# Moving the first outputs' turns to the end of a step in the second kind of heads

## The reference

```python
o_a = diff_attention(q_a, ka_all, va_all, lam)
o_a = rmsnorm(o_a, lw['subln_a']) * (1.0 - l_init)
o_c = softmax_attention(q_c, kc_all, vc_all)
o_b = b_b * conv
y = jnp.concatenate([o_a, o_b, o_c], axis=-1) @ lw['w_out']
```

## Time and profile before

| what | value |
|---|---|
| median of three runs | 2001.78 us |
| the profiled execution, its own time | 2002.92 us |
| its span, first to last instruction | 2000.9 us |
| mean granted TensorE clock | 0.970 |
| PE busy | 1843.9 us, 92% of the span |
| DVE busy | 1407.7 us, 70% |
| ACT busy | 1029.8 us, 51% |
| POOL busy | 333.8 us, 17% |

### The profile page before, as it was taken

How to read it: one execution, slowest core, us unless ns; L and a number is a source line. 1 busy time by engine, 2 the same in 40 slices (tenths; PEclk the granted TensorE clock), 3 DMA queues, 4 the chain that set the end, 5 groups by cost and what they waited for, 6 DMA issues and landing times.

```text
span 2000.9 us, 28755 instructions
## 1 busy us (share of the span) xinstructions
PE 1843.9 (92%) x11276; PEld 1655.3 (83%) x11276; DVE 1407.7 (70%) x2014; ACT 1029.8 (51%) x1401; POOL 333.8 (17%) x507
## 2 busy tenths in 40 slices
PE   5999789799999999998997888897999999999994
PEld 3996777698999999998996776795788888888883
DVE  5487885547666566546477875446988888888887
ACT  4245686524211211124236776434777777777772
POOL 0083540111000000001084531100000000000002
PEclk8999799999999999999998899997999999999997
DMA  9225200023454444421230000007999999999995
GB/s 333 69 94 216 85 1 1 33 74 126 160 168 136 159 138 158 142 80 48 71 100 27 1 1 1 2 22 299 388 405 394 414 403 397 395 392 405 377 387 218
DMA packets 112439, 366.21 MB, mean 183 GB/s; under 512 B 7457, under 2 KB 65217, under 8 KB 85937
## 3 DMA queue, kind: packets, MB, share of 16 engines
q1 hardware_dynamic: 94448, 303.50, 40.5%
q0 software_dynamic: 13536, 48.39, 6.9%
q10 hardware_dynamic: 4320, 12.49, 1.6%
HBM read 349.23 MB, written 15.12 MB: 182 GB/s over the span
## 4 chain that ended last, share of the span: by engine, by line
PE 78%; DVE 9%; ACT 6%; DMA 3%; issue 2%; POOL 1%; SPq 0%; DVEq 0%; POOLq 0%; ACTq 0%
PE PS L2449 28%; PE PS L2338 26%; PE PS L2006 8%; PE PS L2393 5%; PE PS L2430 4%; PE PS L2094 3%; ACT E L909 3%; PE PS L2118 2%; DVE NM L1356 2%; PE PS L2129 2%; ACT PT L914 1%; DVE KCn L1303 1%; DMA araw<-in_w_ada_head 1%; DVE SS L1286 1%; DMA raw<-in_w_ada_head 1%
## 5 line engine op out<-in xcount | busy, mean ns | idle before, releaser
L2449 PEld LDWEIGHTS PS<-H,split 128*128 128x128 f32 x2304 | 339.0, 188 | 2.8 <-issue 1.7
L2449 PE MATMUL PS<-H,split 128*128 128x320 f32 x2304 | 340.7, 310 | 0.5 <-DVE H L1903 0.5
L1088 ACT CAST split<-raw 128x2048 fp32r<-128x2048 f32 (+2 forms) x64 | 112.8, 1763 | 225.9 <-PE PS L2449 174.3
L1550 DVE TENSOR_TENSOR msplit<-raw,msplit 128x2048 fp32r<-128x2048 f32 x82 | 187.9, 2292 | 36.7 <-ACT msplit L1045 36.6
L1639 DVE TENSOR_TENSOR split<-raw,split 128x2048 fp32r<-128x2048 f32 (+2 forms) x64 | 136.5, 2133 | 107.4 <-ACT split L1088 106.9
L1550 DVE TENSOR_TENSOR split<-raw,split 128x2048 fp32r<-128x2048 f32 x82 | 186.8, 2289 | 18.8 <-ACT split L1045 18.8
L2338 PE MATMUL PS<-split,HT 128*128 128x512 f32 x816 | 195.8, 396 | 2.8 <-DVE HT L1529 2.4
L1045 ACT CAST msplit<-raw 128x2048 fp32r<-128x2048 f32 x82 | 157.0, 1915 | 69.9 <-PE PS L2338 61.2
L2338 PE MATMUL PS<-msplit,HT 128*128 128x512 f32 x816 | 191.1, 390 | 1.6 <-DVE msplit L1550 1.6
L2338 PEld LDWEIGHTS PS<-msplit,HT 128*128 128x128 f32 x816 | 152.9, 188 | 34.1 <-DVE msplit L1550 2.4
L2338 PEld LDWEIGHTS PS<-split,HT 128*128 128x128 f32 x816 | 151.9, 189 | 34.1 <-DVE HT L1529 2.8
(11 more groups left out here) (350 smaller groups left out, 3090.9 us busy)
## 6 DMA issues: line engine op xcount, KB each, us to landing
raw<-in_moe_w_gate SPq DMA_DIRECT2D x55, 1024.0 KB, 7.6
raw<-in_moe_w_down SPq DMA_DIRECT2D x55, 1024.0 KB, 8.2
raw<-in_moe_w_up SPq DMA_DIRECT2D x54, 1024.0 KB, 7.5
DOTW<-in_w_ada_rows POOLq DMA_DIRECT2D x56, 512.0 KB, 4.0
raw<-in_w_ada_head SPq DMA_DIRECT2D x16, 1024.0 KB, 6.8
mraw<-in_moe_w_up SPq DMA_DIRECT2D x14, 1024.0 KB, 7.8
mraw<-in_moe_w_gate SPq DMA_DIRECT2D x13, 1024.0 KB, 7.4
mraw<-in_moe_w_down SPq DMA_DIRECT2D x13, 1024.0 KB, 8.4
```

The source lines that it names most:

```text
L1088: A.copy(split[u % 2][:, 0, 0:w], src[:, 0:w]).then_inc(S["split_hi"], 1)
L1550: V.tensor_tensor(msplit[n % M_SPLIT][:, 1, :], mraw[n % M_RAW], msplit[n % M_SPLIT][:, 0, :].bitcast(f32), ALU.subtract).then_inc(S["piec ...
L2449: ins = T.matmul(PS[:, 4 * (u % 2) + 2 * c + hf, 0:HALF], W[:, w, k, c * P:(c + 1) * P], A(a, k, hf), start=(k == 0 and w == 0 and a == 0) ...
```

## The change

In the second kind of heads

- on PE `mix_turn` of tile t stands at the end of step 53 + t, behind the E-turn, and no longer at its start, ahead of the scores;
- on ACT `mix_hi` of tile t stands in step 54 + t behind the copy of `PT`, and no longer at the start of step 53 + t;
- on DVE `mix_lo` of tile t stands at the end of step 54 + t, and no longer at the end of step 53 + t;
- on ACT the cast of the convolution stands at the end of step 52, ahead of all casts of tiles, and no longer at the start of step 58, behind them.

The waits themselves and the work are the same.

```diff
@@ ACT
             for k in range(-2, ITEMS):
                 hg = groups_at(k, 0)
-                if 0 <= k - K_MIX < NT:
-                    mix_hi(k - K_MIX, 1, MIX_A, k - K_MIX)
-                if k == K_MIX + NT:
-                    A.copy(MIX[:, mix_slots(l, 0, MIX_CONV), :], CONV[:, :, :]).then_inc(S["conv_hi"], 1)
                 if k + 2 < ITEMS:
...
                     A.copy(PT[k % 2][:, 0:cols], PSF[:, 3072:3072 + cols]).then_inc(S["pt_out"], 1)
+                if 0 <= k - K_MIX - 1 < NT:
+                    mix_hi(k - K_MIX - 1, 1, MIX_A, k - K_MIX - 1)
                 if (hg := groups_at(k, 1)) is not None:
                     turn_out(*hg)
+                if k == K_MIX - 1:
+                    A.copy(MIX[:, mix_slots(l, 0, MIX_CONV), :], CONV[:, :, :]).then_inc(S["conv_hi"], 1)
@@ DVE
-                if 0 <= k - K_MIX < NT:
-                    mix_lo(k - K_MIX, 1, MIX_A, k - K_MIX)
+                if 0 <= k - K_MIX - 1 < NT:
+                    mix_lo(k - K_MIX - 1, 1, MIX_A, k - K_MIX - 1)
@@ PE
             for k in range(-2, ITEMS + 1):
-                if 0 <= k - K_MIX < NT:
-                    t = k - K_MIX
-                    if t == 0:
-                        pe.wait_ge(S["turn_out"], (l + 1) * TURNS)
-                    else:
-                        pe.wait_ge(S["mix_lo"], l * 10 + t)
-                    pe.wait_ge(S["subln_gained"], l * NT + t + 1)
-                    mix_turn(t, 1, QA[:, t, :])
                 if k + 2 < ITEMS:
...
                     turn_group(*hg)
+                if 0 <= k - K_MIX < NT:
+                    t = k - K_MIX
+                    if t == 0:
+                        pe.wait_ge(S["turn_out"], (l + 1) * TURNS)
+                    else:
+                        pe.wait_ge(S["mix_lo"], l * 10 + t)
+                    pe.wait_ge(S["subln_gained"], l * NT + t + 1)
+                    mix_turn(t, 1, QA[:, t, :])
```

## The result

The changed kernel takes 2023.42 us in the median of four runs (2022.70 to 2026.08), against 2003.04 for the kernel before, which was run once more beside it. The ratio is 1.0105 (95% interval 1.0091 to 1.0119), so it is slower by some 21 us, where 14.5 were forecast. The direction and the two causes, a longer loop of waits and a clock that falls, were right; the clock's share was too small. The forecast time of 2016.3 is 7 us short, and the measured time lies at the upper end of the range, 2023.5 (1.0105 times 2003.04 is 2024.1).

The account below looks back on a forecast made before the run. A loop of waits in attention steps 52 to 59, not a busy engine, was taken as the bound. Loop 3.25 and clock 4.0 us, twice, make 14.5 us on the median of 2001.78: 2016.3 us, range 2007.5 to 2023.5.

Parts of the forecast that it names:

- the loop: Steps 52 to 59: scores, maximum, exponential, copy, cast, remainder, turn, scores; 5.01 us a step, costing 3.25 us a layer.
- The links: Seven waits from scores round to the next scores: 1.28, 0.86, 0.79, 0.59, 0.50, 0.60 and 0.39 us.
- The convolution's cast: ACT, end of step 52: the moved cast is hidden behind the maximum, by 0.1 us only.
- The clock: PE's idle stretches let its clock fall in both layers, between 380 and 387: 4.0 us a layer, bounds 1.95 and 7.5.
- my bound of 7.5: Upper bound a layer if the low clock lasts into the projection: last turns 0.5, `OC` turns 1.2, dense products about 2.
- That the clock holds: Rival for steps 52 to 59: clock stays full, so only the loop's 6.5 us are lost: 2008.3 us; chance 0.18.
- The faster case: Rival: ACT casts the tile ahead of the exponential, so step 53's gain mostly stays: 1.6 us a layer, 1998.6 us; chance 0.05.
- Near-cancellation: Rival: loop binds in steps 55 and 56 only, step 57's wait is hidden: 0 to 3 us, 2003 us; chance 0.07.
- That the convolution's cast does the harm: Rival: the cast at the end of step 52 isn't hidden and delays step 53, adding up to 1.3 us a layer.
- The forecast's own case: Loop and clock together in both layers: 14.5 us slower, bounds 2010.7 to 2023.3 us; chance 0.70.

Follow-up runs that it names:

- filler_full: Changed kernel plus dummy identity turns (8, 16, 20, 10) on PE ahead of the four waits for a tile's remainder: 2009.76 us, ratio 1.0030.
- conv_first_only: Kernel before with only the convolution's cast moved to the end of step 52: 2002.07 us, ratio 0.9997.
- cast_first_remainder_last: Changed kernel with only ACT's tile cast put to the step's start, ahead of the exponential: 1999.28 us, ratio 0.9982; measured again, 2001.16 us, 0.9998.
- conv_back: Changed kernel with the convolution's cast put back to the start of step 58: 2022.04 us, ratio 1.0087.
- cast_first: Changed kernel with ACT's tile cast at the step's start and DVE's remainder right behind the maximum: 2000.99 us, ratio 0.9989.
- before_remainder_early: Kernel before with only DVE's tile remainder moved right behind the maximum of its step: 2002.80 us, ratio 1.0002.
- cast_first_split_late: cast_first with DVE's remainder of the projection's first weights moved from the end of step 55 to that of step 57: 2003.52 us, ratio 1.0004.

## Why the prediction was right or wrong

**The bound and the loop: right.** The links summed to 5.01 us, and filler_full has 5.01. The first steps went as worked through: scores of item 56 3.91 us behind the pair product of step 52 (365.00 to 368.91; 370.83 less 366.87 is 3.96), scores of item 57 8.79 behind it (8.76 worked out), turn of tile 2 13.43 behind it (13.38). PE's waits in layer 0 were 1.33, 2.56, 2.40 and 1.76 us, forecast as 1.3, 2.5, 3.2 and 1.7. The third was shorter only because the scores and turns ahead of it took longer at the lower clock; in layer 1, at full clock, it was 3.30, and its turn came 18.90 us into the stretch (18.78 worked out). The loop's price was forecast at 3.25 us a layer, and it is 3.4.

**The convolution's cast: right**, covered by 0.07 us (0.1 worked out).

**The clock: right that it falls, and mis-sized by a third** (8.0 us forecast, 11.7 measured). This is the step that failed: "So the bounds are 1.95 and 7.5 a layer; I take 4.0". Taking filler_full as the kernel at full clock, layer 0 has 28.26 - 25.34 = 2.9 us in the stretch. From the last pair product to the turns of `OC` it has another 1.5 (4.61 us against 3.13), and from there to the long run of the projection's products another 1.9 (5.27, as 397.87 to 403.14, against 3.37): 6.3 us. Layer 1, in the same way, has 1.6 + 1.5 + 2.3 = 5.4.

What was wrong is that I priced one fall, 6.8 us long as in rows 6, and let it end there. The first fall came about where it was placed: on the time scale of rows 4 it began at 379.9 in layer 0 and at 386.3 in layer 1, where I had said between 380 and 387. It lasted 10.3 us in one and 3.4 in the other. Full clock did come back, at 388.3 in layer 0 and 1289.4 in layer 1. But with the wait ahead of the turn of tile 4 (1.76 us), PE was busy only 1.65 of the next 3.4 us, 1.56 in layer 1, and the clock fell again at 391.7 and 1292.8, for 10.2 us in both layers. This second fall reached through the turns of `OC` into the projection, whose dense work nothing hides. It costs 0.3 + 1.5 + 1.9 = 3.7 us in layer 0 and 1.5 + 2.3 = 3.8 in layer 1; the first costs the remaining 2.6 and 1.6. So 4.0 was too much for the one fall that it priced (3.8 by my terms), and had nothing for the second; the two errors partly cancel, and the number is better than its reason. One price was low as well: the pair product takes 1.1 us more at the lower clock (2.40 for 1.31), where I had 0.95. The parts for the case that the low clock reaches the projection stood in my bound of 7.5, and I left them out.

How a fall comes out isn't fixed by the schedule alone: both layers ran the same work with the same waits up to the turn of tile 2 (13.43 and 13.42 us into the stretch), and the clock fell 13.0 us into the stretch in layer 0 and 19.4 in layer 1. The first fall cost 2.6 us in one and 1.6 in the other, and nothing that I read told which.

The Trainium skill's page "TensorE: Matmul & The Clock Gate" (Part 1: The HAM clock gate) calls the throttled state the default and activity what releases it. The measured term, 11.7 us for both layers, is on the side of that rule; without it the sum would have stopped at the loop's 6.8.

**The sum.** Loop 6.8 and clock 11.7 are 18.5 us. This is what the trace has lost from the pair product of step 52 to the projection, 9.7 us in layer 0 and 8.8 in layer 1, and no second check of it: the clock's part is what the loop leaves over. The span grew by 20.5. The remaining 2 us lie outside, where I expected no change, and I can't tell them from scatter: the two executions already differ by 1.87 us where they reach the stretch, the other way, ahead of anything that was changed, and by some 4 us behind it. What the entry to the experts took (end of the last product of `MIX` to the first of `MAT`) was 91.7 us before, 93.5 after, and 89.7 in conv_first_only.

**The rivals.** That the clock holds is refuted for this kernel, and its time (2008.3) is near what filler_full measured (2009.76). The faster case needed the cast ahead of the exponential; that is cast_first_remainder_last, whose stretch is 1.63 us shorter than before, with 1.6 forecast, so that only ACT's written order kept it away. In whole time this gain is not shown. Near-cancellation, which I placed in the slack of the last short item, is refuted: PE waited the full 1.76 us there. That the convolution's cast does the harm is refuted by conv_back.

**The chances and the range.** The forecast's own case came true, with the clock in the upper half of its bounds (6.3 and 5.4 between 1.95 and 7.5) in both layers. I should have asked of each idle time, and not once for the stretch, whether the clock could fall in it; then a second fall would have stood in the sum, as a bound at least.

## What to carry to other kernels

In a pipeline written out by hand, moving an instruction behind a wait in the same step can close a loop through engines that weren't in it before: write down the new loop link by link and compare its sum with the step, not with the busy times. When the new loop leaves TensorE idle as often as here (waits of 1.3 to 3.3 us, one behind the other), add the clock to the sum, asking at each of them whether it could fall and following a fall up to the next dense work. Give it as bounds: the same waits had different falls in the two layers. To tell the two apart on a chip, fill the idle time with products that nobody reads.

## What the runs showed that I had not expected

- The price of idle time is not steady. An idle time of 1.42 us left the clock at 1.00 in the kernel before (rows 2, and the row below) and in cast_first_remainder_last; the 2.00 us in cast_first and in before_remainder_early were each followed by products at the lower clock (2.00 and 2.40 us for 1.31). And 1.56 us in cast_first_split_late were followed by a fall in layer 1 and by none in layer 0. Which other work lay around them differs too, so this is no threshold, only where it fell.
- Therefore a shorter loop can be slower: before_remainder_early cuts 0.58 us a step and ends 0.5 us later in layer 0 and 0.3 in layer 1.
- Full clock can come back between two falls and not stay: in the changed kernel the low clock lasted from 378.0 to 388.3 and again from 391.7 to 401.9.
- Whole times of one kernel scatter over 5 to 18 us here, from the lowest to the highest of ten or more, while the stretch repeats to 0.02 us from one execution to another at full clock. A gain of 3 us in the stretch could be read from the trace and not from the times.

The row of the kernel before that the first point rests on, its wait ahead of the turn of tile 4:

```profile
383.41 0.55 PE L2393 MATMUL PS<-ident,QA 128*128 128x128 f32 x3 [1.42 <-DVE MIX L1334]
```
